# Dilated mixer: contiguous query blocks, two heads a step, and a softmax joined from two tables

## The reference, cut to what matters

```python
sc = einsum('bchnqd,bchnkd->bchnqk', qs, ks) + bias[:, None]
sc = where(mask, sc, NEG_INF)
lse = logsumexp(sc, axis=-1)
pr = exp(sc - lse[..., None])
o = einsum('bchnqk,bchnkd->bchnqd', pr, vs)
...
wts = softmax(stack(lses, axis=0), axis=0)
o = sum(wts[..., None] * stack(outs, axis=0), axis=0)
```

## Time and profile before

| | us |
|---|---|
| median of 3 runs (2146.7 to 2149.95) | 2148.03 |
| the profiled execution's own time | 2147.91 |
| its span, first to last instruction | 2146.1 |
| TensorE busy (98% of the span), 9198 matmul records | 2098.9 |
| TensorE's weight loads (78%) | 1671.8 |
| GpSimd busy (65%) | 1387.4 |
| VectorE busy (35%) | 747.5 |
| ScalarE busy (24%) | 509.6 |

### The profile page before, as it was taken

One profiled execution on the slowest core, in us unless ns is written; L12 is line 12 of the kernel. 1 busy time (PEld: TensorE's weight loads), 2 busy tenths in 40 slices (PEclk: granted clock), 3 DMA queues, 4 the chain that ended last, 5 costly groups with the idle time before them and its releaser, 6 DMA issues.

```text
span 2146.1 us, 29009 instructions
## 1 busy us (share of the span) xinstructions
PE 2098.9 (98%) x9198; PEld 1671.8 (78%) x9198; DVE 747.5 (35%) x1230; ACT 509.6 (24%) x923; POOL 1387.4 (65%) x1372
## 2 busy tenths in 40 slices
PE   8999999999999999999999999999899999999997
PEld 6877866778888888878888887877667778888885
DVE  3133355443210122352222135355664552221024
ACT  2032243331210121241110012244652422110011
POOL 6633333367776777667777778655677467777675
PEclk9999999999999999999999999999999999999998
DMA  6411111122222232222223234222222122223221
GB/s 232 141 59 40 49 40 56 53 79 98 97 93 95 97 108 98 92 86 97 98 98 98 97 99 166 89 69 69 89 79 98 49 69 94 94 96 98 98 98 59
DMA packets 56403, 193.85 MB, mean 90 GB/s; under 512 B 6383, under 2 KB 8687, under 8 KB 55956
## 3 DMA queue, kind: packets, MB, share of 16 engines
q1 hardware_dynamic: 52220, 184.05, 25.8%
q10 hardware_dynamic: 4120, 8.95, 1.3%
HBM read 190.85 MB, written 5.27 MB: 91 GB/s over the span
## 4 chain that ended last, share of the span: by engine, by line
PE 93%; DVE 3%; ACT 2%; issue 1%; DMA 0%; SPq 0%; DVEq 0%; ACTq 0%
PE acc L271 26%; PE acc L273 26%; PE acc L272 26%; PE st L317 2%; PE ob L649 1%; PE sc L634 1%; PE ob L462 1%; PE sc L475 1%; PE sc L1500 1%; PE sc L477 1%; PE acc L861 1%; PE acc L859 1%; PE tp L642 1%; PE acc L860 1%; DVE arena L1619 1%
## 5 line engine op out<-in xcount | busy, mean ns | idle before, releaser
L1712 POOL TENSOR_TENSOR w_lo<-w_raw,w_hi 128x512 fp32r<-128x512 f32 x684 | 922.9, 1349 | 57.1
L1710 POOL TENSOR_SCALAR w_hi<-w_raw 128x512 fp32r<-128x512 f32 x684 | 466.8, 682 | 681.0 <-PE acc L273 636.6
L271 PE MATMUL acc<-h_hi,w_hi 128*128 128x512 f32 x1864 | 749.3, 402 | 14.1 <-DVE h_lo L1852 8.9
L273 PE MATMUL acc<-h_hi,w_lo 128*128 128x512 f32 x1864 | 727.3, 390 | 0.0
L272 PE MATMUL acc<-h_lo,w_hi 128*128 128x512 f32 x1864 | 727.0, 390 | 0.0
L271 PEld LDWEIGHTS acc<-h_hi,w_hi 128*128 128x128 f32 x1864 | 351.1, 188 | 103.5 <-issue 23.4
L272 PEld LDWEIGHTS acc<-h_lo,w_hi 128*128 128x128 f32 x1864 | 351.2, 188 | 81.2 <-issue 10.1
L273 PEld LDWEIGHTS acc<-h_hi,w_lo 128*128 128x128 f32 x1864 | 350.8, 188 | 74.2
L271 PE MATMUL acc<-hid_hi,w_hi 128*128 128x512 f32 x608 | 236.9, 390 | 0.0
L272 PE MATMUL acc<-hid_lo,w_hi 128*128 128x512 f32 x608 | 236.6, 389 | 0.0
L273 PE MATMUL acc<-hid_hi,w_lo 128*128 128x512 f32 x608 | 236.5, 389 | 0.0
(11 more groups left out here) (265 smaller groups left out, 1921.8 us busy)
## 6 DMA issues: line engine op xcount, KB each, us to landing
w_raw<-in_wstream SPq DMA_DIRECT2D x341, 512.0 KB, 3.5
x<-in_xT SPq DMA_DIRECT2D x8, 256.0 KB, 5.3
bias_skew<-bias_rows ACTq DMA_DIRECT2D x4, 512.0 KB, 8.2
out_y<-x SPq DMA_DIRECT2D x8, 256.0 KB, 2.2
arena<-bias_skew ACTq DMA_DIRECT2D x4, 257.5 KB, 3.3
bias_skew<-bias_rows ACTq DMA_DIRECT2D x4, 256.0 KB, 8.7
arena<-in_memT ACTq DMA_DIRECT2D x1, 1024.0 KB, 7.5
arena<-in_decay ACTq DMA_DIRECT2D x1, 1024.0 KB, 10.7
```

The source lines that it names most:

```text
L271: nc.tensor.matmul(dst, w_hi[:, slot, k, :], xh[:, k, :], start=first, stop=False)
L273: done = nc.tensor.matmul(dst, w_lo[:, slot, k, :], xh[:, k, :], start=False, stop=last)
L1710: nc.gpsimd.tensor_scalar(w_hi[:, slot, ks, :], w_raw[:, raw, ks, :], 1.0, 0.0, ALU.mult, ALU.add).then_inc(w_rounded, 1)
L1712: nc.gpsimd.tensor_tensor(w_lo[:, slot, ks, :], w_raw[:, raw, ks, :], w_hi[:, slot, ks, :].bitcast(F32), ALU.subtract).then_inc(w_split, 1)
```

## The change

The steps become 8: head pair c = 0, 1 and block b = 0..3, two joint heads a step. In group 0 a block is now the 128 contiguous tokens from 128 b, and its keys are a span of 256 that contains the band (`B_KEYS`, from key 0, 64, 192 or 256). Groups 1 and 2 keep the token classes: class b has its 128 queries and 128 keys. The two heads of a pair lie in partitions 0 to 63 and 64 to 127; their score matmuls alternate, each head into its own bank, 256 + 128 + 128 columns.

Queries of group 0 and of groups 1 and 2 are thus in different orders, and the one softmax is split in two: type 0 (band) and type 1 (classes), each with its own minimum and sum (the scores are negated, so a minimum stands for the maximum) in columns of a table `tab`. The value products stay unnormalised, 64 columns for each head and type, and ScalarE copies them to `osb`. Once for each head pair, TensorE carries the other type's table entries to each token's row through two 128x128 permutations (`perm`, a new input of 128x264 values), VectorE picks them out (`b_spread_dve`, `b_other_dve`), computes the weight of each type (`b_join_dve`, with an exponential by ScalarE, `b_weight_act`) and scales both types' outputs. Both are transposed (`b_out_pe`, eight transposes a pair); ScalarE copies the band's (`b_x_act`) and VectorE adds the classes' in token order (`b_add_dve`).

Further: the value transposes move between the last eight units of `b_proj`, and become 30, since spans that begin at 64 or 192 need values with an offset of 64 (`v_off`). Transposes of the probabilities and their copies go head by head, 4 a head. The position rows shrink from 1536 columns to 1024 and are made in one place; the skewed tables shrink with them. lambda's matmul moves after unit 8. The units of `a_proj` are spread by `B_UNITS`. The first `pv` of mixer A waits for `b_add` at 2, and two semaphore counters of later stages lose the dilated mixer's 16. The diff, without declarations and mixer A's counter changes:

```diff
-ROW0, ROW1 = 1024, 256
-SKEW0 = ROW0 - 4
-W_BIAS0 = SEQ + 3
+ROW0, ROW1 = 512, 256
+SKEW0 = ROW0 - 1
+W_BIAS0 = 384
+B_KEYS = [0, 64, 192, 256]
+B_BIAS = [128, 64, 64, 0]
...
+        V_TURN = [(0, 0), (0, 1), (1, 0), (1, 1), (2, 0), (3, 0), (4, 0), (5, 0)]
+        def b_v_turn_pe(pe, k):
+            c, off = V_TURN[k]
+            pe.wait_ge(s("b_v"), counted(k - 1))
+            for t in range(4 - off):
+                v = v_raw(c)[:, 64 * off + t * P:64 * off + (t + 1) * P] if c < 2 else every4(v_raw(c), t)
+                m = nc.tensor.transpose(tp[k % 2][:, t * P:(t + 1) * P], v, ident)
+            m.then_inc(s("b_vtr"), 1)
...
+        B_UNITS = {0: [2], 1: [3], 2: [4], 3: [5], 4: [6, 7], 5: [8], 6: [9, 10], 7: [11]}
+        B_ROPE = {1: 0, 2: 1, 3: 2, 4: 3}
+        def b_pv_pe(pe, st_):
+            c, b = divmod(st_, 4)
+            o = ob[:, 0:256]
+            pe.wait_ge(s("b_os"), st_)
+            for hd in range(2):
+                h = slice((2 * c + hd) * 64, (2 * c + hd) * 64 + 64)
+                pe.wait_ge(s("b_cp"), 2 * st_ + hd + 1)
+                for t in range(2):
+                    nc.tensor.matmul(o[:, hd * 64:hd * 64 + 64], pT_b[hd][:, t * P:(t + 1) * P], b_window(b, t)[:, h],
+                                     start=t == 0, stop=t == 1)
+                for g in range(1, 3):
+                    m = nc.tensor.matmul(o[:, P + hd * 64:P + hd * 64 + 64], pT_b[hd][:, (g + 1) * P:(g + 2) * P],
+                                         vb_tok[:, g, b, h], start=g == 1, stop=g == 2)
+                m.then_inc(s("b_pv"), 1)
+        def b_perm_pe(pe, c):
+            pe.wait_ge(s("a_rot_used"), 4)
+            pe.wait_ge(s("b_add"), c)
+            pe.wait_ge(s("b_mix"), CMB * c + 2)
+            pe.wait_ge(s("perm_in"), 16)
+            nc.tensor.matmul(st[:, 0:64], perm_s[:, P:2 * P], own_ex[:, 0:64], start=True, stop=True)
+            nc.tensor.matmul(st[:, 64:P], perm_s[:, 0:P], own_ex[:, 64:P], start=True, stop=True).then_inc(s("b_pm"), 1)
+        def b_out_pe(pe, c, t, to):
+            pe.wait_ge(s("b_mix"), CMB * (c + 1))
+            pe.wait_ge(s("b_x"), c + t)
+            for b in range(4):
+                m = nc.tensor.transpose(to[:, b * P:(b + 1) * P], osb[t][:, c, 2 * b:2 * b + 2].rearrange("p h d -> p (h d)"), ident)
+            m.then_inc(s("b_otr"), 1)
+        def b_x_act(act, c, of):
+            act.wait_ge(s("b_otr"), 2 * c + 1)
+            nc.scalar.copy(ob_T[:, c, :], of).then_inc(s("b_x"), 1)
+        def b_add_dve(dve, c, of):
+            to = ob_T[:, c, :].rearrange("p (j r) -> p r j", r=4)
+            dve.wait_ge(s("b_otr"), 2 * c + 2)
+            nc.vector.tensor_tensor(to, of.rearrange("p (r j) -> p r j", r=4), to, ALU.add).then_inc(s("b_add"), 1)
         def mixer_b_pe(pe):
             def score(st_):
-                r, i = divmod(st_, 4)
-                p0 = 64 * (i % 2)
+                c, b = divmod(st_, 4)
+                pe.wait_ge(s("b_tt"), 4 * st_)
                 for g in range(3):
-                    if g == 0:
-                        nc.tensor.matmul(sc_w[:, 0:512], every4(q, r), k, start=True, stop=True)
+                    for hd in range(2):
+                        q = z_b(2 * g + c)[64 * hd:64 * hd + 64]
+                        k = z_b(6 + 2 * g + c)[64 * hd:64 * hd + 64]
+                        if g == 0:
+                            nc.tensor.matmul(sc[hd][:, 0:256], q[:, b * P:(b + 1) * P], k[:, B_KEYS[b]:B_KEYS[b] + 256],
+                                             start=True, stop=True)
+                        else:
+                            m = nc.tensor.matmul(sc[hd][:, (g + 1) * P:(g + 2) * P], every4(q, b), every4(k, b),
+                                                 start=True, stop=True)
...
+            for st_ in range(8):
+                if st_ < 7:
+                    score(st_ + 1)
+                if st_ in B_ROPE:
+                    rope_stat_pe(pe, B_ROPE[st_])
+                if st_ == 5:
+                    b_perm_pe(pe, 0)
+                if st_ == 7:
+                    b_out_pe(pe, 0, 1, st[:])
+                n = B_UNITS[st_][0]
+                out1(pe, "a_proj", n, n % 2, h1_hi, h1_lo)
+                if st_ in B_ROPE:
+                    rope_turn_pe(pe, B_ROPE[st_])
+                if st_ == 6:
+                    b_out_pe(pe, 0, 0, st[:])
                 if st_:
                     b_pv_pe(pe, st_ - 1)
+                for n in B_UNITS[st_][1:]:
+                    out1(pe, "a_proj", n, n % 2, h1_hi, h1_lo)
+                for hd in range(2):
+                    pe.wait_ge(s("b_pr"), 4 * st_ + 2 * hd + 2)
+                    pe.wait_ge(s("b_cp"), counted(2 * st_ + hd - 1))
+                    for kt in range(4):
+                        m = nc.tensor.transpose(tp[hd][:, kt * P:(kt + 1) * P], pS[st_ % 2][hd][:, kt * P:(kt + 1) * P], ident)
...
             def exp(st_):
+                c, b = divmod(st_, 4)
+                for hd in range(2):
+                    for t in range(2):
+                        act.wait_ge(s("b_tt"), 4 * st_ + 2 * hd + t + 1)
+                        p = pS[st_ % 2][hd][:, 256 * t:256 * t + 256]
+                        nc.scalar.activation(p, p, ACT.Exp, bias=tab_of(c, t, 0, hd, b), scale=-1.0,
+                                             accum_out=tab_of(c, t, 1, hd, b)).then_inc(s("b_pr"), 1)
...
+        def b_join_dve(dve, c):
+            dve.wait_ge(s("b_wx"), c + 1)
+            nc.vector.tensor_tensor(w(3), w(1), tc[:, 1], ALU.mult).then_inc(s("b_mix"), 1)
+            nc.vector.tensor_tensor(w(4), w(2), oc[:, 1], ALU.mult).then_inc(s("b_mix"), 1)
+            ...
+            for t in range(2):
+                o = osb[t][:, c]
+                nc.vector.tensor_tensor(o, o, own_w[:, 112 + 8 * t:120 + 8 * t].unsqueeze(2).to_broadcast([P, 8, 64]),
+                                        ALU.mult).then_inc(s("b_mix"), 1)
...
@@ mixer A, TensorE
             def pv(h):
                 pe.wait_ge(turned_copy, TILES0["full"] + 4 * h + 4)
                 pe.wait_ge(s("a_lo"), h)
+                pe.wait_ge(s("b_add"), 2)
...
+                if h == 0:
+                    b_out_pe(pe, 1, 0, ob[:])
                 out1(pe, "gates", 2 * h + 1, 1, h1_hi, h1_lo)
+                if h == 0:
+                    b_out_pe(pe, 1, 1, ob[:])
@@ mixer A, VectorE
                 scaled1(dve, "gates", 2 * h, gate_z(2 * h))
+                if h == 0:
+                    b_join_dve(dve, 1)
...
                 if h + 4 < 10:
                     rope_dve(dve, h + 4)
+                if h == 0:
+                    b_add_dve(dve, 1, ob[:])
@@ TensorE's main line
-            out1(pe, "b_proj", 3, 1, h1_hi, h1_lo)
-            pe.wait_ge(s("row_copied"), 2)
-            out_loop(pe, "b_proj", 4, 18, h1_hi, h1_lo)
+            for n in range(3, 18):
+                out1(pe, "b_proj", n, n % 2, h1_hi, h1_lo)
+                if n == 8:
+                    pe.wait_ge(s("row_copied"), 2)
+                    pe.wait_ge(s("lam_prod"), 1)
+                    nc.tensor.matmul(sc[1][:, 0:2], ones, lam_t[:, 0:2], start=True, stop=True).then_inc(s("lam_sum"), 1)
+                if n >= 10:
+                    b_v_turn_pe(pe, n - 10)
```

More of the change, by code:

```diff
@@ L77 @@
 MUL0 = {"f1in_a": 1, "f1in_b": 17, "f2in_a": 23, "f2in_b": 39}
-WIDE0 = {"dilated": 0, "full": 16, "diff": 48, "mem": 80}
-TILES0 = {"dilated": 0, "full": 16, "diff": 48, "mem": 64}
+WIDE0 = {"full": 0, "diff": 32, "mem": 64}
+TILES0 = {"full": 0, "diff": 32, "mem": 48}
 GAINS = {}
@@ L445, in b_o_copy_act @@
[L445 to L456, removed]
-            r, i = divmod(st_, 4)
-            pe.wait_ge(turned_copy, st_ + 1)
-            pe.wait_ge(s("b_on"), st_)
-            for kt in range(6):
-                v = vb_tok[:, 0, kt, i * 64:(i + 1) * 64] if kt < 4 else vb_tok[:, kt - 3, r, i * 64:(i + 1) * 64]
-                m = nc.tensor.matmul(ob[:, i * 64:(i + 1) * 64], pT_b[st_ % 2][:, kt * P:(kt + 1) * P], v,
-                                     start=kt == 0, stop=kt == 5)
-            m.then_inc(s("b_pv"), 1)
+        V_TURN = [(0, 0), (0, 1), (1, 0), (1, 1), (2, 0), (3, 0), (4, 0), (5, 0)]
@@ L506, in mixer_b_pe @@
-                pe.wait_ge(s("b_v"), 6)
-                for kt in range(6):
-                    m = nc.tensor.transpose(tp_w[:, kt * P:(kt + 1) * P], pS[st_ % 2][:, kt * P:(kt + 1) * P], ident)
-                m.then_inc(turned, 1)
-                if i == 0 and r > 0:
-                    b_o_turn_pe(pe, r - 1)
+                for n in B_UNITS[st_][1:]:
[5 more added lines that the diff above has]
+                        m = nc.tensor.transpose(tp[hd][:, kt * P:(kt + 1) * P], pS[st_ % 2][hd][:, kt * P:(kt + 1) * P], ident)
+                    m.then_inc(s("b_tr"), 1)
@@ L580, in mixer_b_dve @@
-            b_norm(15)
+                if st_ in B_ROPE:
+                    stat_v_dve(dve, item_stat(B_ROPE[st_]), HD_A)
+                if st_ == 5:
```

(14 more changed lines are left out.)

264 lines of the change are left out of this document (145 added, 119 removed).

## The result

| | before | after |
|---|---|---|
| median, us | 2148.99 (2146.7 to 2153.17, 4 runs) | 2114.38 (2112.47 to 2115.32, 4 runs) |
| profiled execution | 2147.91 | 2113.47 |
| its span | 2146.1 | 2111.7 |
| TensorE's matmul records | 9198 | 9122 |

The change makes the kernel faster: 0.9836 of the time before, 95% interval 0.9818 to 0.9853, 34.6 us by the medians. I had forecast 2128.7 us, a gain of 19.3, with a range that ended at 2118. (A fourth run of the kernel before moves its median from the 2148.03 shown above to 2148.99.)

The account below looks back on a forecast made before the run. The prediction took TensorE as the bound (98% busy, 93% of the chain). Its terms, -11.8 - 7.9 - 3.6 + 0 - 1.1 + 2.1 - 1.2 + 2.5 + 1.7 = -19.3 us, took 2148.0 to 2128.7, range 2118 to 2137.

Parts of the forecast that it names:

- scores: Dilated mixer's score matmuls on TensorE: 33.4 us in 16 steps become 21.6 in 8, -11.8.
- value products: Dilated mixer's value matmuls on TensorE: 23.7 us become 15.8 by the count of passes at 0.123 each, -7.9.
- transposes of probabilities: TensorE transposes in the dilated mixer's steps: 10.6 us become 7.0, -3.6.
- values to token order, lambda: Value transposes moved between projection units 10 to 17, lambda's waits gone: together 0, between -1 and +1.
- position rows: Position-row matmuls, in two places before, become one 512-column and two 256-column products with one re-entry less: -1.1.
- joining and output: Output transposes, sixteen for eight, +0.9, and tables through TensorE twice, +1.2: together +2.1 us.
- waits, gone and added: TensorE waits: two gone, -1.2; added before the full mixer's first value product and behind `b_join_dve`, together +2.5.
- clock: Lower-clock spells in the mixer: three instead of two, by new stretches of about 5.5 us; +1.7, between -3.4 and +8.5.
- If only the moving passes overlap: Case taken for two heads' scores: passes overlap, strided loads come one after another; 2.7 us a step, 21.6 in all.
- full overlap: Score case where the two heads' loads overlap too: 1.8 us a step, 14.2 in all; chance 0.29.
- -10.2: End of the score range with nothing overlapping between the two heads: 2.9 us a step, 23.2 in all.
- the rival's, 2121.3: Rival time if the halves overlap with their loads: scores 14.2 us instead of 21.6, whole 2121.3; chance 0.29.

Follow-up runs that it names:

- Experiment 1: Changed kernel with both heads of a pair reading queries and keys from partitions 0 to 63 (second head's output wrong): 2131.6 us, 0.9938 of before.
- experiment 6: Changed kernel with VectorE's addition of the second pair (`b_add`) ahead of head 4's rope instead of behind it: 2106.99 us, single run.
- experiment 5: Changed kernel with VectorE writing queries and keys of groups 1 and 2 in class order, so 128-column scores read contiguously: 2110.03 us, 0.9834 of before.
- experiment 7: Changed kernel with VectorE's join of the second pair ahead of the scaling of gates unit 0 instead of behind it: 2109.9 us, single run.
- experiment 2: Changed kernel with each step's score matmuls queued head 0 first, then head 1, instead of alternating: 2116.9 us, 0.9876 of before.
- experiment 8: Changed kernel with one 16-column VectorE addition (sum of the joint weights) writing every other column of a free table: 2110.78 us, single run.
- experiment 9: Changed kernel with all eight groups of value transposes after the last projection unit instead of between units: 2113.11 us, 0.9851 of before.

## Why the prediction was too small

Term by term, by the two traces:

| term | forecast | measured |
|---|---|---|
| scores | -11.8 | -21.0 (33.4 to 8 x 1.55 = 12.4) |
| value products | -7.9 | -9.8 (23.7 to 8 x 1.74 = 13.9) |
| transposes of probabilities | -3.6 | -3.6 |
| values to token order, lambda | 0 | -0.6 |
| position rows | -1.1 | -1.0 |
| joining and output | +2.1 | +1.4 (4 x 0.22 to 4 x 0.44 + 0.36 + 0.17) |
| waits, gone and added | +1.3 | +2.6 (-1.5, +4.1) |
| clock | +1.7 | -3.4 (-1.7 in the mixers, -1.7 in the second block) |
| sum | -19.3 | -35.4; the spans differ by 34.4 |

**The step that failed is that of the scores.** I had written: "If only the moving passes overlap, three slots of 0.216 stand for four and the strided loads still come one after another: 2.7 a step", and took it "because the row shows these scores bound by the load and not by the pass". The row shows a load of 318 ns; it doesn't show whether two can run at once. Runs show that they do. 1.55 a step is even below the 1.8 that I had for full overlap, since a pair takes the time of one: six passes of one head, 2 x 0.216 and 4 x 0.23, are 1.35, and 0.2 of entry make the 1.55. I had counted n + 1 slots for the 2n passes of n matmuls, and it is n. Experiment 1 puts 11.0 us on the overlap alone; the other 10 of the 21.0 are the smaller count of columns, which I had (-10.2).

**And the evidence was there.** I had written that "no row of before shows such a pair side by side", and that was wrong. The second block's scores at L1277 are of 64 partitions, in two halves, into two banks. The timeline of the kernel before there, and the chain over the same matmuls:

```profile
1504.52 1.13 PE L1277 MATMUL sc<-arena 64*128 64x512 f32 x4
```

```profile
1504.59 1.06 PE sc L1277 x4
```

Four 512-column passes in 1.06, where four over all 128 partitions take 1.72 (`248.87 1.72` in experiment 6), 0.43 each. Of the second block I had used only the row of its 256-column scores. The loads of this row are contiguous (186 ns), so it doesn't show that strided ones pair as well. By that row the forecast would have been the rival's, 2121.3, and with a pair in the time of one (8 x 0.25 less), 2119.3. The chance of 0.29 for the overlap was too low, and the sentence about the rule of the Trainium skill (TensorEngine Tiling, Key Properties), by which tiles load and multiply in parallel, is confirmed: 1.55 against 2.92 in one half.

**Value products** were sized a little too long: 1.74 a step, 0.109 a pass against my 0.123, which held the entry of a group of 12. I had named this (-8.3) and not taken it.

**Values to token order** gave -0.6 for my 0. One reading was off: from 114.53 + 0.23 to 115.36 are 0.6 us and not 0.8, and the last pass of the unit is still among them.

**The waits** stood where I put them and were longer: 2.9 for 2.3 and 1.2 for 0.2. The addition took 1.05 and not 0.69 to 0.92; it reads `ob` in one order and writes in another, as the scaling by classes does that takes 1.09 in experiment 5, but no run tests this alone. The statistic's wait was longer by one instruction of 16 columns that took 1.23 and not 0.18, beside GpSimd's split: I had left GpSimd out of the sum, and those 1.05 us are what was missing. Experiments 6 and 7 take each away, with 2.9 and 1.0.

**The clock** had the wrong sign. I counted spells by stretches of 5.5 us; with scores at 1.55 they became 4.2, and no step has a spell. Experiment 1, where the stretches have the 5.5 that I had assumed, shows five spells where I counted three, but two of them without such a stretch, so the rule that I counted by isn't borne out either. The 1.7 in the second block is the same code in both kernels and varies from run to run; I count it to neither. It is these windows (before, then after):

```profile
1510.00:1520.00 10.00, 6.95 (x41) 5.34 (x42) 8.78 (x20) 6.24 (x14) 6.66 (x7) 0.88 0.26 83
1520.00:1530.00 10.00, 9.49 (x45) 7.67 (x44) 5.07 (x17) 4.98 (x14) 4.04 (x4) 0.78 0.16 53
```
```profile
1460.00:1470.00 10.00, 8.54 (x50) 6.00 (x49) 7.70 (x23) 6.39 (x18) 6.55 (x6) 0.96 0.16 52
1470.00:1480.00 10.00, 9.64 (x61) 7.87 (x60) 4.53 (x14) 6.51 (x15) 6.18 (x7) 0.87 0.33 105
```

Without it the sum is -33.7. The trace can check this: the first pass of gates unit 2, behind all that the change touches, starts at 258.35 us instead of 291.79, 33.4 earlier. The rest of the way to 34.4 is code that is the same in both kernels: about 1.1 us lost near 1265 us, where TensorE waits for a split of GpSimd, about 1.2 won of the 1.7 in the second block's clock, and 0.9 won in the last statistic (1.11 instead of 2.06, at the lower clock before).

**Right**: TensorE as the bound (busy -37.3 for a span -34.4), the transposes, the position rows, no wait inside the eight steps, units of the same length, and the place of both new waits.

## What to carry to other kernels

Before pricing two small matmuls in separate row halves, search the whole trace for any line with `64*128` and a count of passes whose chain time is below passes x slot: one such row tells whether they run at once. When matmuls are short, both their operands are to be contiguous, and an engine that is idle can put them so while it writes them anyway. When an instruction frees a bank that TensorE wants, put it ahead of longer work on its own queue: two lines moved on VectorE gave 4.8 us here in one profile.

## What was not expected of the hardware

- fp32 scores in two row halves run wholly at once, loads and passes: eight 128-column passes in 0.44 us contiguous, 0.92 with every fourth column; in one half 0.89 and 1.86.
- TensorE takes a pass of the free half from four places further back in the queue (experiment 2).
- Either operand alone, if it is strided by four fp32, holds a pair at 0.82 to 0.91.
- A VectorE addition of 16 columns, both operands in SBUF, took 1.22 or 1.23 us the 24 times that it began inside GpSimd's split of weights, and ended with it; it took 0.18 the two times that it met none (experiment 8). An instruction that is short by its size is to be checked against GpSimd's timeline before it is priced.
- Spells of the lower clock lasted 3.4 us and took 1.7 each. They came in five of the eight steps of experiment 1 (scores of 2.92 us), in two of the sixteen of the kernel before (2.09), in none with scores of 1.95 or less, and behind the wait of 2.9 us in all profiles that have it but those of experiments 1, 7 and 9. What decides is open.
